# Full down projections of a hybrid encoder by a seven-product block scheme on one Trainium2 core

## The chip, the core and the metric

The kernel runs on one core of one Trainium2 chip (trn2). The metric is device time in microseconds: 1104.0 us before, the median of 3 runs (1103.97 to 1104.03). Every duration below is read from one profiled execution, unless it is said to be this median.

## What is computed

A bidirectional encoder trunk of two layers on 512 tokens of 1024 features in float32. The change touches the feed-forward half of a layer alone:

```python
h = _rmsnorm(x, g_ffn[l])
z = _dwconv_centred(h @ w_up[l], conv_w[l], conv_b[l])
z_gate, z_val = jnp.split(z, [D_FF], axis=-1)
x = x + (jax.nn.silu(z_gate) * z_val) @ w_down[l]
```

D_FF is 2816, 22 tiles of 128 features. The convolution is over three neighbouring tokens. The first half of a layer (projections, spatial gating, gated linear attention, output projection) and the final norm are as before.

## The kernel before

All activations lie feature-major: 128 features of a tile on the partitions, 512 tokens along them. A weight "slab" is 128 x 1024 float32, 8 blocks of 128 x 128, of which one projection tile needs a whole one. Every float32 product is three products in the type fp32r, high x high, high x low and low x high (`three`, lines 1042 to 1046), accumulated in one of four PSUM banks `acc0` to `acc3`. A slab goes through four slots j = 0 to 3, in this order: SP loads it to `w_raw` once the low part of the slab before it in the slot is made (`load_slab`); ACT copies it to `w_hi` (`split_hi`, line 348) once the array has finished with the slot; POOL subtracts (line 339) to get `w_lo` and counts `lo_done`; PE waits for `lo_done` and multiplies.

The 22 feature tiles are done in three parts: two full parts of 8 tiles and a last one of 6. A full part has 16 up slabs, in four groups of four (`up_quad` on ACT and DVE; two feature tiles each, gate and value), and then 8 down slabs, whose products are 8 blocks deep and 512 columns wide. Per up slab DVE scales the bank into `y` (line 940, a PSUM bank), ACT makes the centre tap (line 600), DVE adds the two outer taps (line 949). Per tile ACT takes the silu (line 608), DVE multiplies into `gated`, in PSUM (line 954), ACT copies it to `feat_hi` or `feat2_hi` (line 611) and DVE subtracts for the low part (line 931). Per down slab DVE adds the bank to `x` (`add_to_x`, line 915). `project_pair` interleaves the first two down slabs so that the last tiles' features are wanted late.

The order of each engine's work is written out by hand; semaphores with absolute counts tie the engines. Each engine takes its own instructions strictly in that order, so a wait holds back everything behind it on its engine.

In the printed source below, the projection's heart is:

```python
pe.matmul(out, wh, ah, start=first, stop=False)
pe.matmul(out, wh, al, start=False, stop=False)
return pe.matmul(out, wl, ah, start=False, stop=last)
```

## Time and profile before

| | |
|---|---|
| median of 3 runs | 1104.0 us (1103.97 to 1104.03) |
| span of the profiled execution | 1102.4 us |
| PE busy | 1092.6 us (99%), 5328 products |
| PE weight loads | 905.8 us (82%) |
| DVE busy | 531.0 us (48%) |
| ACT busy | 484.7 us (44%) |
| POOL busy | 464.8 us (42%) |
| HBM read | 105.98 MB, 98 GB/s over the span |

The profiled execution's own time is its span, first to last instruction of the program; it is 1.6 us below the median of the runs, which have the launch around it too. Busy time is the union of an engine's records; products overlap in the array, so two starts tell their pace and one record's length does not. Times in the timeline views count from the start of the span.

### The profile page before, as it was taken

To read this page: it belongs to the slowest core of one execution; us is meant where nothing else is said; L and a number is where in the kernel's file an instruction comes from. 1 tells how busy PE (TensorE), PEld (TensorE's weight loads), DVE (VectorE), ACT (ScalarE), POOL (GpSimd) and SP (SyncE) were. 2 spreads that over 40 slices of the span, in tenths; PEclk is the share of its full clock that TensorE was granted. 3 is DMA by queue.
4 is the path that set the end of the run, shared out by engine and by line. 5 is a ranking of instruction groups with operands and counts; after the bars stand their busy time and mean duration, and the time that the engine had idled before them with its cause. 6 is when DMAs were issued, how large, how long until landed. Compare 5 with 4: busy or idle time off the path is not lost.

```text
span 1102.4 us, 16315 instructions
## 1 busy us (share of the span) xinstructions
PE 1092.6 (99%) x5328; PEld 905.8 (82%) x5328; DVE 531.0 (48%) x816; ACT 484.7 (44%) x656; POOL 464.8 (42%) x202
## 2 busy tenths in 40 slices
PE   9999999999999999999999999999999999999997
PEld 7788888888888888888878888888888888888886
DVE  5726755655215551255536368456541355314545
ACT  7835444454225441344557344346432454313451
POOL 5334234344534443544634332435444444444450
PEclk9999999999999999999999999999999999999999
DMA  8222223232222222222522212222332322232222
GB/s 301 93 96 78 68 76 105 78 109 100 96 95 94 97 96 95 96 96 97 180 97 81 91 63 74 95 77 96 115 95 76 115 96 95 79 117 91 96 77 78
DMA packets 33607, 108.79 MB, mean 99 GB/s; under 512 B 3984, under 2 KB 6800, under 8 KB 33552
## 3 DMA queue, kind: packets, MB, share of 16 engines
q1 hardware_dynamic: 32848, 107.03, 29.2%
q10 hardware_dynamic: 704, 1.07, 0.3%
q8 instruction: 30, 0.49, 0.2%
q14 instruction: 25, 0.20, 0.1%
HBM read 105.98 MB, written 2.10 MB: 98 GB/s over the span
## 4 chain that ended last, share of the span: by engine, by line
PE 97%; DVE 1%; DMA 1%; ACT 0%; POOL 0%; SPq 0%; issue 0%; DVEq 0%
PE acc L1044 28%; PE acc L1045 28%; PE acc L1046 28%; PE acc L1170 3%; PE acc L1171 3%; PE acc L1172 3%; PE side L1140 1%; PE side L1258 1%; PE side L1242 1%; DMA x<-xT 1%; PE side L1248 1%; PE side L1221 1%; DVE arena L1019 1%; PE side L1201 1%; PE acc L1132 0%; PE acc L1121 0%
## 5 line engine op out<-in xcount | busy, mean ns | idle before, releaser
L339 POOL TENSOR_TENSOR w_lo<-w_raw,w_hi 128x1024 fp32r<-128x1024 f32 x188 | 453.4, 2416 | 600.6 <-ACT w_hi L348 600.6
L1044 PE MATMUL acc<-xg_hi,w_hi 128*128 128x512 f32 x864 | 338.8, 392 | 0.0
L1045 PE MATMUL acc<-xg_lo,w_hi 128*128 128x512 f32 x864 | 336.3, 389 | 0.0
L1046 PE MATMUL acc<-xg_hi,w_lo 128*128 128x512 f32 x864 | 336.2, 389 | 0.0
L348 ACT ACTIVATE w_hi<-w_raw 128x1024 fp32r<-128x1024 f32 x190 | 200.0, 1057 | 255.2 <-PE acc L1046 219.2
L1044 PEld LDWEIGHTS acc<-xg_hi,w_hi 128*128 128x128 f32 x864 | 162.2, 188 | 35.8 <-issue 2.0
L1046 PEld LDWEIGHTS acc<-xg_hi,w_lo 128*128 128x128 f32 x864 | 162.2, 188 | 33.9
L1045 PEld LDWEIGHTS acc<-xg_lo,w_hi 128*128 128x128 f32 x864 | 162.2, 188 | 33.5 <-issue 0.5
L1044 PE MATMUL acc<-feat_hi,w_hi 128*128 128x512 f32 (+1 forms) x492 | 188.9, 384 | 0.0
L1045 PE MATMUL acc<-feat_lo,w_hi 128*128 128x512 f32 (+1 forms) x492 | 188.8, 384 | 0.0
L1046 PE MATMUL acc<-feat_hi,w_lo 128*128 128x512 f32 (+1 forms) x492 | 188.8, 384 | 0.0
L949 DVE SCALAR_TENSOR_TENSOR arena<-side,conv_sb,arena 128x511 f32<-128x511 f32 x176 | 132.0, 750 | 116.8 <-ACT arena L600 104.0
L600 ACT ACTIVATE arena<-side,conv_sb 128x512 f32<-128x512 f32 x88 | 68.5, 778 | 127.7 <-DVE side L940 126.7
L915 DVE TENSOR_TENSOR x<-x,acc 128x512 f32 (+1 forms) x62 | 42.4, 685 | 167.8 <-PE acc L1046 167.8
L940 DVE TENSOR_TENSOR side<-acc,rstdT 128x512 f32<-128x512 f32 x88 | 61.4, 698 | 97.6 <-PE acc L1046 95.4
L1045 PEld LDWEIGHTS acc<-feat_lo,w_hi 128*128 128x128 f32 x492 | 92.4, 188 | 18.3
L1044 PEld LDWEIGHTS acc<-feat_hi,w_hi 128*128 128x128 f32 x492 | 92.4, 188 | 18.3
L1046 PEld LDWEIGHTS acc<-feat_hi,w_lo 128*128 128x128 f32 x492 | 92.4, 188 | 18.2
L611 ACT ACTIVATE feat_hi<-side 128x512 f32 (+1 forms) x44 | 26.4, 599 | 81.0 <-DVE side L954 81.0
L678 DVE SCALAR_TENSOR_TENSOR xg_lo<-x,gains_sb,xg_hi 128x512 fp32r<-128x512 f32 x32 | 41.5, 1306 | 29.6 <-ACT xg_hi L357 29.5
L1170 PE MATMUL acc<-w_hi,xg_hi 128*128 128x512 f32 x128 | 50.2, 392 | 0.0
L1171 PE MATMUL acc<-w_hi,xg_lo 128*128 128x512 f32 x128 | 49.8, 389 | 0.0
(131 smaller groups left out, 803.2 us busy)
## 6 DMA issues: line engine op xcount, KB each, us to landing
w_raw<-slabs SPq DMA_DIRECT2D x190, 512.0 KB, 3.3
outT<-arena SPq DMA_DIRECT2D x7, 256.0 KB, 2.3
ln_sb<-ln_gb SPq DMA_DIRECT2D x2, 512.0 KB, 7.7
w_raw<-slabs SPq DMA_DIRECT2D x4, 128.0 KB, 4.6
x<-xT ACTq DMA_DIRECT2D x2, 256.0 KB, 4.6
x<-xT SPq DMA_DIRECT2D x2, 256.0 KB, 5.9
x<-xT ACTq DMA_DIRECT2D x1, 512.0 KB, 7.2
w_raw<-slabs SPq DMA_DIRECT2D x2, 256.0 KB, 6.9
```

The source lines that it names most:

```text
L339: pool.tensor_tensor(w_lo[:, w], w_raw[:, w], w_hi[:, w].bitcast(F32), ALU.subtract).then_inc(lo_done, 1)
L348: act.activation(w_hi[:, w], w_raw[:, w], ACT.Copy).then_inc(hi_done, 1)
L600: act.activation(z[j], y[j], ACT.Identity, scale=conv_sb[:, bass.ds(coef + 1, 1)], bias=conv_sb[:, bass.ds(coef + 3, 1)]).then_inc(centre_ ...
L678: dve.scalar_tensor_tensor(out=xg_lo[:, w], in0=x[:, w], scalar=gains_sb[:, bass.ds(r * KT + m, 1)], in1=xg_hi[:, w].bitcast(F32), op0=ALU ...
L915: dve.tensor_tensor(x[:, bass.ds(m * S, S)], x[:, bass.ds(m * S, S)], acc[j][:, :], ALU.add).then_inc(x_done, 1)
L940: dve.tensor_tensor(y[j], acc[j][:, :], rstdT[:, :], ALU.mult).then_inc(y_ready, 1)
L949: dve.scalar_tensor_tensor(out=to, in0=of, scalar=conv_sb[:, bass.ds(coef + tap, 1)], in1=to, op0=ALU.mult, op1=ALU.add).then_inc(taps_don ...
L1044: pe.matmul(out, wh, ah, start=first, stop=False)
L1045: pe.matmul(out, wh, al, start=False, stop=False)
L1046: return pe.matmul(out, wl, ah, start=False, stop=last)
L1170: pe.matmul(acc[t][:, :], ah, wh, start=(k == 0), stop=False)
L1171: pe.matmul(acc[t][:, :], al, wh, start=False, stop=False)
```

## The change

The two full parts' down projections, in both layers, go through Strassen's scheme in Winograd's form. Eight down slabs are two quads of four. The host repacks each quad's weights (`quad_major`), so that its four slabs are the blocks of a 2 x 2 scheme: input tiles even or odd, output tiles of one or the other of a pair. The activations are split the same way: even and odd feature tiles, first and second half of the tokens (H = 256). Each quad then takes 7 "units" instead of 8 block products. A unit is 4 tile pairs x 2 output tiles x 3 products of 256 columns, 24 products; a part has 14 units, counted by `unit_done`. The second half of unit 4 and the last quarter of unit 3 are written apart: unit 4's first half stands before unit 3.

New operands have to be made:
- of the weights, per quad: S1 = block 1 + block 3, S2 = S1 - block 0, block 0 - block 1, S4 = block 2 - S2, each 128 x 1024. In the first quad POOL makes S1 and S2 and DVE the other two; in the second DVE makes all four. Each unit's block gets its own high part (ACT) and low part (POOL), so a part has 14 low parts in place of 8.
- of the features, per pair of tiles: T1 (DVE, from a copy that ACT makes, 256 columns), T2, T3, T4 (DVE, 256 columns each), a high part of T1 and one of T2 to T4 (ACT, 256 and 768 columns), and their low parts (DVE). The odd tile's low part and that of T2 to T4 stand behind the next pair's first scaling (`odd_low`); for the last pair they stand behind the first unit's addition.

S1 and S4 lie in `mixer_sb`, S2 in `sum_s2`. Blocks 1 and 3 of the second quad are loaded early into free places of `arena` (`second_raw`). DVE adds each finished unit into the one, two or four quarters of `x` that it belongs to (`add_unit`), some of them before the same bank goes on accumulating.

```diff
+        second_raw = {1: slot(4, 2), 3: slot(6, 2)}
+        t_raw, even_copy = slot(20, 2), slot(22)[:, 0:H]
...
+                    for j in second_raw:
+                        load(j, second_loaded[j])
                     for j in range(RING):
-                        load_slab(L, q, j)
+                        sp.wait_ge(lo_done, n + j + 1)
+                        if j in second_raw:
+                            sp.sem_inc(raw_loaded[j], 16)
+                        else:
+                            load(j, raw_loaded[j])
...
-            with pool.Fori(1, DEPTH * NS // RING) as q:
-                for j in range(RING):
-                    w = slice(j * SLAB, (j + 1) * SLAB)
-                    pool.wait_ge(hi_done, q * RING + (j + 1))
-                    pool.tensor_tensor(w_lo[:, w], w_raw[:, w], w_hi[:, w].bitcast(F32),
-                                       ALU.subtract).then_inc(lo_done, 1)
...
+            def low_quads(L, part):
+                m, slab = quads_at(L, part)
+                n = L * NS + slab
+                pool.wait_ge(hi_sum, 6 * m + 1)
+                low(0, raw(0)).then_inc(lo_sum, 1)
+                pool.wait_ge(raw_loaded[1], 16 * (n // RING) + 16)
+                pool.wait_ge(raw_loaded[3], 16 * (n // RING) + 16)
+                if m:
+                    pool.wait_ge(sum_done, 6 * m)
+                pool.tensor_tensor(sum_s1, raw(1), raw(3), ALU.add).then_inc(sum_done_pool, 1)
+                pool.wait_ge(sum_done_pool, 2 * m + 1)
+                pool.tensor_tensor(sum_s2[:, :], sum_s1, raw(0), ALU.subtract).then_inc(sum_done_pool, 1)
+                pool.wait_ge(hi_sum, 6 * m + 2)
+                low(1, sum_s1).then_inc(lo_sum, 1)
+                pool.wait_ge(hi_done, n + 1)
+                pool.wait_ge(sum_done, 6 * m + 2)
+                low(2, sum_s2[:, :]).then_inc(lo_done, 1)
+                pool.wait_ge(hi_sum, 6 * m + 3)
+                low(3, raw(2)).then_inc(lo_sum, 1)
+                pool.wait_ge(hi_done, n + 2)
+                low(0, raw(1)).then_inc(lo_done, 1)
+                pool.wait_ge(hi_done, n + 3)
+                low(1, sum_s4).then_inc(lo_done, 1)
+                pool.wait_ge(hi_done, n + 4)
+                low(2, raw(3)).then_inc(lo_done, 1)
...
+                    on_its_own(act)
+                    act.activation(even(H), t_raw[:, 0:H], ACT.Copy).then_inc(t_hi_done, 1)
+                    if down is None:
+                        next_hi(2)
+                    else:
+                        act.wait_ge(sum_done_pool, 2 * m + 2)
+                        unit_hi(2, sum_s2[:, :], hi_done)
+                    silu(1)
+                    if down is None:
+                        centre(1, 1)
+                        next_hi(3)
+                    else:
+                        act.wait_ge(acc_ready, L * NS + slab + RING)
+                        raw_at(2, first)
+                        unit_hi(3, raw(2), hi_sum)
+                        centre(1, 1)
+                        act.wait_ge(unit_done, 14 * m + 1)
+                        act.wait_ge(sum_done, 6 * m + 2)
+                        unit_hi(0, raw(1), hi_done)
+                    act.wait_ge(t_done, stage * 2 + 2)
+                    on_its_own(act)
+                    act.activation(odd, gated[1], ACT.Copy).then_inc(feat_hi_done, 1)
+                    act.activation(t_of, t_raw[:, H:4 * H], ACT.Copy).then_inc(t_hi_done, 1)
...
+                def odd_low(part, k):
+                    hi, lo = pair_parts(k)
+                    t_at = slice(k * 3 * H, (k + 1) * 3 * H)
+                    stage = L * (FULL_PARTS * KP) + part * KP + k
+                    dve.wait_ge(feat_hi_done, L * NF + part * KT + (KT + 2 * k + 2))
+                    dve.tensor_tensor(lo(S, S), gated[1], hi(S, S).bitcast(F32), ALU.subtract).then_inc(feat_ready, 1)
+                    dve.wait_ge(t_hi_done, stage * 2 + 2)
+                    dve.tensor_tensor(t_lo[:, t_at], t_raw[:, H:4 * H], t_hi[:, t_at].bitcast(F32),
+                                      ALU.subtract).then_inc(t_ready, 1)
...
+                    scale(0)
+                    if k:
+                        odd_low(part, k - 1)
+                    taps(0, 0)
+                    scale(1)
+                    taps(0, 1)
+                    gate(0)
+                    if k == KP - 1:
+                        dve.wait_ge(sum_done_pool, 2 * m + 2)
+                        dve.wait_ge(raw_loaded[2], 16 * (L * (NS // RING)) + 4 * first + 16)
+                        dve.tensor_tensor(sum_s4, raw(2), sum_s2[:, :], ALU.subtract).then_inc(sum_done, 1)
+                    scale(2)
+                    dve.wait_ge(feat_hi_done, L * NF + part * KT + (KT + 2 * k + 1))
+                    dve.tensor_tensor(lo(0, H), gated[0][:, 0:H], hi(0, H).bitcast(F32),
+                                      ALU.subtract).then_inc(feat_ready, 1)
+                    dve.wait_ge(even_copied, stage + 1)
+                    dve.tensor_tensor(t1, gated[0][:, H:S], even_copy, ALU.subtract).then_inc(t_done, 1)
+                    taps(1, 0)
+                    dve.wait_ge(t_hi_done, stage * 2 + 1)
+                    dve.tensor_tensor(lo(H, H), t1, hi(H, H).bitcast(F32), ALU.subtract).then_inc(t_ready, 1)
+                    scale(3)
+                    if k == KP - 1:
+                        dve.tensor_tensor(raw(1), raw(0), raw(1), ALU.subtract).then_inc(sum_done, 1)
+                    taps(1, 1)
+                    gate(1)
+                    dve.wait_ge(gated_done, f + 2)
+                    dve.tensor_tensor(t2, gated[1][:, H:S], t1, ALU.subtract).then_inc(t2_done, 1)
+                    dve.wait_ge(t2_done, stage + 1)
+                    dve.tensor_tensor(t4, gated[1][:, 0:H], t2, ALU.subtract)
+                    dve.tensor_tensor(t3, t2, gated[0][:, 0:H], ALU.subtract).then_inc(t_done, 1)
...
+                    add_unit(0, 0, 0, 0, units + 1, unit_added)
+                    odd_low(part, KP - 1)
+                    add_unit(0, 1, 1, 1, units + 2, unit_added)
+                    dve.wait_ge(second_loaded[1], 16 * m + 16)
+                    dve.wait_ge(second_loaded[3], 16 * m + 16)
+                    dve.wait_ge(lo_sum, 6 * m + 2)
+                    dve.tensor_tensor(sum_s1, second_raw[1], second_raw[3], ALU.add).then_inc(sum_done, 1)
+                    add_unit(0, 0, 1, 0, units + 3, unit_added)
+                    dve.wait_ge(raw_loaded[0], loads)
+                    dve.tensor_tensor(second_raw[1], raw(0), second_raw[1], ALU.subtract).then_inc(sum_done, 1)
+                    add_unit(0, 0, 0, 2, units + 4, x_done, added + 1)
+                    dve.wait_ge(sum_done, 6 * m + 3)
+                    dve.wait_ge(lo_done, n + 1 + RING)
+                    dve.tensor_tensor(sum_s2[:, :], sum_s1, raw(0), ALU.subtract).then_inc(sum_done, 1)
+                    add_unit(0, 0, 1, 1, units + 5, x_done, added + 3)
+                    dve.wait_ge(raw_loaded[2], loads)
+                    dve.wait_ge(sum_done, 6 * m + 5)
+                    dve.wait_ge(lo_done, n + 3 + RING)
+                    dve.tensor_tensor(sum_s4, raw(2), sum_s2[:, :], ALU.subtract).then_inc(sum_done, 1)
+                    add_unit(0, 1, None, 0, units + 6, x_done, added + 2)
+                    dve.wait_ge(x_done, L * NX + part * KT + (KT + RING + 3))
+                    add_unit(0, 1, 0, 2, units + 7, x_done)
...
+                def unit(bank, slot_of, pairs, moving, first):
+                    for k in pairs:
+                        for r in range(2):
+                            a = slot_of * SLAB + r * (SLAB // 2) + k * P
+                            xh, xl = moving(k)
+                            out = acc[bank][:, r * H:(r + 1) * H]
+                            pe.matmul(out, w_hi[:, a:a + P], xh, start=(first and k == 0 and r == 0), stop=False,
+                                      skip_group_check=True)
+                            pe.matmul(out, w_hi[:, a:a + P], xl, start=False, stop=False, skip_group_check=True)
+                            last = pe.matmul(out, w_lo[:, a:a + P], xh, start=False, stop=(k == KP - 1),
+                                             skip_group_check=True)
+                    return last
...
+                    pe.wait_ge(lo_sum, 6 * m + 1)
+                    pe.wait_ge(y_ready, ys + 1)
+                    pe.wait_ge(feat_ready, feats + KT - 1)
+                    unit(0, 0, every_pair, b11, True).then_inc(unit_done, 1)
+                    pe.wait_ge(lo_sum, 6 * m + 2)
+                    pe.wait_ge(y_ready, ys + 2)
+                    pe.wait_ge(t_ready, stages + 2 * KP - 1)
+                    unit(1, 1, every_pair, t1, True).then_inc(unit_done, 1)
+                    pe.wait_ge(lo_sum, 6 * m + 3)
+                    pe.wait_ge(y_ready, ys + 3)
+                    unit(2, 3, range(0, 2), b21, True)
+                    pe.wait_ge(lo_done, n + 1)
+                    pe.wait_ge(unit_added, 6 * m + 1)
+                    unit(0, 2, range(0, 3), t2, False)
+                    pe.wait_ge(t_ready, stages + 2 * KP)
+                    unit(0, 2, range(3, 4), t2, False).then_inc(unit_done, 1)
+                    pe.wait_ge(feat_ready, feats + KT)
+                    unit(2, 3, range(2, 4), b21, False).then_inc(unit_done, 1)
+                    pe.wait_ge(lo_done, n + 3)
+                    pe.wait_ge(unit_added, 6 * m + 2)
+                    unit(1, 1, every_pair, b22, False).then_inc(unit_done, 1)
+                    pe.wait_ge(unit_added, 6 * m + 3)
+                    unit(0, 0, every_pair, t3, False).then_inc(unit_done, 1)
+                    pe.wait_ge(lo_done, n + 4)
+                    pe.wait_ge(x_done, xs + 1)
+                    unit(2, 2, every_pair, t4, True).then_inc(unit_done, 1)
...
+    def quad_major(w, rows, m):
+        v = w[rows.start:rows.stop, m * P:(m + RING) * P].reshape(KP, 2, P, 2, 2, P)
+        return [v[:, odd, :, :, i].transpose(1, 2, 0, 3).reshape(P, SLAB) for odd in range(2) for i in range(2)]
```

**On POOL, at the first quad's start.** Before, one loop of four low parts runs from one end of the program to the other. A piece of it:

```order
L339 TENSOR_TENSOR w_lo<-w_raw,w_hi 128x1024 [waits hi_done]
L338 REGISTER_ALU
L339 TENSOR_TENSOR w_lo<-w_raw,w_hi 128x1024 [waits hi_done]
L335 REGISTER_ALU
L335 COMPARE_AND_BRANCH
```

Now, from the last pair of up tiles on:

```order
L399 TENSOR_TENSOR w_lo<-w_raw,w_hi 128x1024 [waits hi_sum]
L410 TENSOR_TENSOR mixer_sb<-w_raw 128x1024 [waits raw_loaded3,raw_loaded1]
L412 TENSOR_TENSOR sum_s2<-mixer_sb,w_raw 128x1024 [waits sum_done_pool]
L399 TENSOR_TENSOR w_lo<-mixer_sb,w_hi 128x1024 [waits hi_sum]
L399 TENSOR_TENSOR w_lo<-sum_s2,w_hi 128x1024 [waits sum_done,hi_done]
L399 TENSOR_TENSOR w_lo<-w_raw,w_hi 128x1024 [waits hi_sum]
L399 TENSOR_TENSOR w_lo<-w_raw,w_hi 128x1024 [waits hi_done]
L399 TENSOR_TENSOR w_lo<-mixer_sb,w_hi 128x1024 [waits hi_done]
L399 TENSOR_TENSOR w_lo<-w_raw,w_hi 128x1024 [waits hi_done]
```

The two sums stand between the low parts of units 1 and 2, and the low part of S2 (the fifth row) waits for `sum_done`, DVE's count of its own two sums.

**On DVE, in the last pair of up tiles, around the third tile's scaling.** Before:

```order
L954 TENSOR_TENSOR side1<-side0,arena 128x512 [waits silu_done]
L939 REGISTER_ALU
L940 TENSOR_TENSOR side2<-acc2,rstdT 128x512 [waits acc_ready]
L930 ISA
L931 ISA [waits feat_hi_done]
L931 TENSOR_TENSOR feat2_lo<-side1,feat2_hi 128x512
```

Now:

```order
L1220 TENSOR_TENSOR side1<-side0,arena 128x512 [waits silu_done]
L1230 ISA
L1231 ISA [waits sum_done_pool]
L1232 TENSOR_TENSOR mixer_sb<-w_raw,sum_s2 128x1024 [waits raw_loaded2]
L1203 REGISTER_ALU
L1204 TENSOR_TENSOR side2<-acc2,rstdT 128x512 [waits acc_ready]
L1234 REGISTER_ALU
L1235 TENSOR_TENSOR feat2_lo<-side1,feat2_hi 128x256 [waits feat_hi_done]
L1237 REGISTER_ALU
L1238 TENSOR_TENSOR arena<-side1,arena 128x256 [waits even_copied]
```

The sum S4 (line 1232), which waits for POOL's S2, has come between the gate of the first tile and the scaling of the third up slab.

## Rows read from the trace of the kernel before

**Rows 1.** The page: span, PE's busy time, chain by engine.

```profile
span 1102.4 us, 16315 instructions
...
PE 1092.6 (99%) x5328; PEld 905.8 (82%) x5328; DVE 531.0 (48%) x816; ACT 484.7 (44%) x656; POOL 464.8 (42%) x202
...
PE 97%; DVE 1%; DMA 1%; ACT 0%; POOL 0%; SPq 0%; issue 0%; DVEq 0%
```

**Rows 2.** Busy time by stretches (the first line names the columns).

```profile
core 0: us, PE busy (x) PEld busy (x) DVE busy (x) ACT busy (x) POOL busy (x), PEclk, DMA share, GB/s
...
234.13:277.66 43.53, 43.53 (x193) 36.04 (x192) 22.87 (x32) 18.61 (x24) 19.46 (x9) 1.00 0.29 97
277.66:321.18 43.52, 43.52 (x193) 36.04 (x192) 8.40 (x12) 9.53 (x10) 19.07 (x8) 1.00 0.30 100
```

**Rows 3.** Timeline of PE at 1081.8 (start, us, engine, line, tiles).

```profile
1081.77 0.39 PE L1046 MATMUL acc<-feat_hi,w_lo 128*128 128x512 f32 x1
1081.99 0.28 PE L1044 MATMUL acc<-feat_hi,w_hi 128*128 128x256 f32 x1
1082.11 0.28 PE L1045 MATMUL acc<-feat_lo,w_hi 128*128 128x256 f32 x1
```

**Rows 4.** Timelines of PE, DVE, ACT and POOL from 277.6 to 284.

```profile
277.66 0.39 PE L1044 MATMUL acc<-feat_hi,w_hi 128*128 128x512 f32 x1
...
277.86 0.70 DVE L940 TENSOR_TENSOR side<-acc,rstdT 128x512 f32<-128x512 f32 x1 [1.86 <-PE acc L1046]
279.80 1.64 DVE L949 SCALAR_TENSOR_TENSOR arena<-side,conv_sb,arena 128x511 f32<-128x511 f32 x2 [1.24 <-ACT arena L600]
281.56 0.70 DVE L954 TENSOR_TENSOR side<-side,arena 128x512 f32<-128x512 f32 x1
283.22 0.69 DVE L931 TENSOR_TENSOR feat_lo<-side,feat_hi 128x512 f32 x1 [0.96 <-ACT feat_hi L611]
...
278.88 0.78 ACT L600 ACTIVATE arena<-side,conv_sb 128x512 f32<-128x512 f32 x1 [2.24 <-DVE side L940]
279.56 1.04 ACT L348 ACTIVATE w_hi<-w_raw 128x1024 fp32r<-128x1024 f32 x1
282.46 0.60 ACT L611 ACTIVATE feat_hi<-side 128x512 f32 x1 [1.86 <-DVE side L954]
...
280.68 2.40 POOL L339 TENSOR_TENSOR w_lo<-w_raw,w_hi 128x1024 fp32r<-128x1024 f32 x1 [3.04 <-ACT w_hi L348]
```

**Rows 5.** Groups by line and shape, and the page's DMA row.

```profile
L339 POOL TENSOR_TENSOR w_lo<-w_raw,w_hi 128x1024 fp32r<-128x1024 f32 x188 | 453.4, 2416 | 600.6 <-ACT w_hi L348 600.6
...
L348 ACT ACTIVATE w_hi<-w_raw 128x1024 fp32r<-128x1024 f32 x190 | 200.0, 1057 | 255.2 <-PE acc L1046 219.2
...
L915 DVE TENSOR_TENSOR x<-x,acc 128x512 f32<-128x512 f32 x30 | 20.4, 681 | 36.7 <-PE acc L1046 36.7
...
L991 DVE TENSOR_TENSOR x<-x,acc 128x256 f32<-128x256 f32 x4 | 1.7, 420 | 0.7 <-PE acc L1046 0.6
...
w_raw<-slabs SPq DMA_DIRECT2D x190, 512.0 KB, 3.3
```

**Rows 6.** Timelines of DVE and POOL at 141 and at 158.

```profile
141.71 2.47 DVE L880 TENSOR_TENSOR feat_lo<-arena,feat_hi 128x512 fp32r<-128x512 f32 x1 [0.92 <-ACT feat_hi L553]
...
158.57 2.29 DVE L678 SCALAR_TENSOR_TENSOR xg_lo<-x,gains_sb,xg_hi 128x512 fp32r<-128x512 f32 x1 [1.26 <-ACT xg_hi L357]
...
161.38 0.67 DVE L915 TENSOR_TENSOR x<-x,acc 128x512 f32<-128x512 f32 x1
...
141.24 2.40 POOL L339 TENSOR_TENSOR w_lo<-w_raw,w_hi 128x1024 fp32r<-128x1024 f32 x1 [5.74 <-ACT w_hi L348]
...
157.91 5.22 POOL L339 TENSOR_TENSOR w_lo<-w_raw,w_hi 128x1024 fp32r<-128x1024 f32 x2 [7.92 <-ACT w_hi L348]
```

**Rows 7.** Busy time by stretches at the end, PE's timeline at the start.

```profile
1098.50:1100.00 1.50, 0.00 (x0) 0.00 (x0) 0.50 (x2) 0.00 (x0) 0.00 (x0) 1.00 1.03 340
1100.00:1102.40 2.40, 0.00 (x0) 0.00 (x0) 0.00 (x0) 0.00 (x0) 0.00 (x0) 0.51 0.32 105
...
1.64 1.70 PE L1088 MATMUL side<-ones_r 128*128 128x128 f32 x7
...
4.74 1.73 PE L1088 MATMUL side<-ones_r 128*128 128x128 f32 x14
```

More of the change, by code:

```diff
@@ L52 @@
 HALVES = (slice(0, S // 2), slice(S // 2, S))
+H = S // 2
+KP = KT // 2
+QUADS = KT // RING
 TAIL = (KT - 2, KT - 1)
@@ L243, in on_its_own, with raw, raw_of, quads_at @@
             eng.sem_inc(waits_passed, 1)
+        def raw(j):
+            return w_raw[:, j * SLAB:(j + 1) * SLAB]
+        def raw_of(g, j):
+            return second_raw[j] if g and j in second_raw else raw(j)
+        def quads_at(L, part):
+            return L * FULL_PARTS + part, part * PART + (N_FFN + 2 * KT)
         def load_x(eng, g):
@@ L334, in _, with low_slabs @@
                                    ALU.subtract).then_inc(lo_done, 1)
-            with pool.Fori(1, DEPTH * NS // RING) as q:
-                for j in range(RING):
-                    w = slice(j * SLAB, (j + 1) * SLAB)
-                    pool.wait_ge(hi_done, q * RING + (j + 1))
-                    pool.tensor_tensor(w_lo[:, w], w_raw[:, w], w_hi[:, w].bitcast(F32),
-                                       ALU.subtract).then_inc(lo_done, 1)
+            def low_slabs(L, first, end):
+                with pool.Fori(L * (NS // RING) + first // RING, L * (NS // RING) + end // RING) as q:
+                    for j in range(RING):
+                        pool.wait_ge(hi_done, q * RING + (j + 1))
+                        low(j, raw(j)).then_inc(lo_done, 1)
@@ L343, in _ @@
+            for L in range(DEPTH):
+                before = RING if L == 0 else 0
+                for part in range(FULL_PARTS):
+                    low_slabs(L, before, N_FFN + part * PART + 2 * KT)
+                    low_quads(L, part)
+                    before = N_FFN + (part + 1) * PART
+                low_slabs(L, before, NS)
         @block.scalar
@@ L966, in _ @@
+                with dve.Fori(0, FULL_PARTS) as part:
+                    for k in range(KP):
+                        up_pair(part, k)
+                    down_quads(part)
                 for q in range(LAST_TILES // 2):
@@ new lines, in part_of, with moving, t_part @@
+                def part_of(odd, half):
+                    def moving(k):
+                        w = slice(half * H, (half + 1) * H)
+                        return tuple(featT(hi, 2 * k + odd)[:, w] for hi in (True, False))
+                    return moving
+                def t_part(i):
+                    def moving(k):
+                        a = k * 3 * H + (i - 2) * H
+                        return t_hi[:, a:a + H], t_lo[:, a:a + H]
+                    return moving
+                b11, t1, b21, b22 = part_of(0, 0), part_of(0, 1), part_of(1, 0), part_of(1, 1)
@@ L1355, in _ @@
                     if part < FULL_PARTS:
-                        with pe.Fori(0, KT // RING) as q:
-                            for j in (1, 2, 3):
-                                down_tile(j, q, *places)
+                        down_quads(part)
                     else:
@@ L1447 @@
             rows = range(tiles.start * P, tiles.stop * P)
-            slabs += [channel_major(w_down[l], rows, m * P) for m in range(KT)]
+            if len(tiles) == KT:
+                for m in range(0, KT, RING):
+                    slabs += quad_major(w_down[l], rows, m)
+            else:
+                slabs += [channel_major(w_down[l], rows, m * P) for m in range(KT)]
     slabs = np.stack(slabs)
```

248 lines of the change are left out of this document (223 added, 25 removed).

## The prediction

> **What bounds the kernel now.** I read the page first: TensorE is busy 99% of a span of 1102.4 us and 97% of the chain that ended last is PE [rows 1]. The other engines have slack on average, so a change pays only through the array's own work or through a wait that it makes. Next, the busy time by stretches around the first full part's down projections in layer 0 [rows 2]: four pairs of up tiles end at 277.66, the eight down tiles take 277.66 to 321.18, 43.52 us, and the array never stops in either. 43.52 over 8 x 24 products is 0.2267 us for one of 512 columns; an up tile is 5.44 us. There are four such down stretches. POOL is busy only 19.07 of the 43.52 us, 8 low parts of 2.4 us. Then the array's own timeline where it goes from 512 to 256 columns [rows 3]: starts are 0.22 apart before and 0.12 after, while a record reads 0.39 and 0.28, so starts count.
>
> **The product saving.** The change replaces 192 products of 512 columns by 14 units of 24 products of 256 columns, 336. At the pitch of [rows 3] a unit is 24 x 0.12 = 2.88 us, a stretch 40.32 us: 3.20 us less than 43.52, 12.8 us over four. This is the whole gain; it would give 1091.2. The Trainium skill ("TensorE: Matmul & The Clock Gate", Back-to-back issue gap) gives N/2.4 + 2.5 ns, 215.8 and 109.2: by it the estimate would be 41.4 - 36.7 = 4.7 us a stretch. The rows have some 13 ns on top of N/2.4 at both widths, so shorter products gain less, and the rows decide.
>
> **Durations and handoffs.** POOL 2.42 mean for 1024 columns, ACT 1.06 for a high part, DVE 0.68 for 512 and 0.42 for 256 columns [rows 5]. I extrapolate DVE: 0.94 for 768, 1.20 for 1024. At the end of an up tile [rows 4] DVE begins 0.20 after the array, ACT 0.3 after DVE, DVE 0.14 after ACT, POOL 0.08 after ACT; centre 0.78, two taps 1.64, gate 0.70, low part 0.69.
>
> **The hold.** What this trace shows of DVE beside POOL decides the rest [rows 6]. A subtraction on DVE with both inputs in SBUF began at 141.71 while POOL was in an operation that began at 141.24 and took 2.40: it took 2.47 instead of 0.68, ending 0.54 after POOL. Another, from 158.57 to 160.86, ended 0.55 after POOL's first operation (157.91 + 2.4), and POOL's next ended later for it: the two read 5.22 together instead of 4.8. An addition with one input in PSUM, at 161.38 in the middle of a POOL operation, took its usual 0.67. So such a DVE operation and a POOL operation follow one another, whole. The new DVE work holds many of that kind: the block sums (1024 columns), T1's low part (256), the T2-T4 low part (768). I charge: wait for POOL's end, then the duration less 0.14; POOL's next starts behind it.
>
> **Entry into the first quad**, time 0 being the end of the last up tile (277.66 in the old trace).
> - The third pair ends late. Its fourth up tile ended at -21.76; scaling waits for T1's low part, itself held behind POOL's low part (about 0.7). Then centre, taps, gate as in [rows 4], and three new 256-column differences: -15.3. ACT makes the odd high part 0.60 and the T high part 0.83: -13.6. Centre and w_hi for unit 1, 0.78 + 1.05: -11.7.
> - POOL, in its new order, has four operations of 2.40: low of block 0 (-9.2), S1 (-6.8), S2 (-4.4), low of S1 (-2.0). The low of S1 stands ready behind S2, so POOL goes straight on.
> - DVE waits for S2 at the sum S4, and everything of the pair is queued behind. S2 exists at -4.4, but POOL is already in the low of S1: S4 ends at -2.0 + 1.06 = -0.9. The scaling of tile 3, due at -5.24, ends at -0.2; the even low part at 0.2 (unit 1 starts 0.3 late); T1 0.6; ACT's centre to 0.84; taps 2.6; T1's low 3.0; scaling of tile 4 3.7; raw0 - raw1 5.0.
> - POOL may take the low of S2 only after that difference: 7.5, then the low of raw2: 10.0. The array is through units 1 and 2 at 0.3 + 5.76 = 6.1 and needs the low of raw2: it goes on at 10.2. **Wait 4.1 us**, in sum 4.4.
> - Odd high part, T high part and, held once more, the T2-T4 low part end at about 13.2, due in unit 3's last quarter at 13.8; with no wait before it that would be due at 9.4, so it is next in line.
>
> **Through the quads.** From 5.2 POOL owes nine low parts before unit 10 (S2, raw2, raw1, S4, raw3; raw0, S1, raw2, S2): 21.6 us. Between them DVE puts the 768-column low part and four sums (held each time): 0.8 + 4 x 1.07 = 5.1; POOL saves 0.14 of its start at each, 0.7. Together 5.2 + 21.6 + 5.1 - 0.7 = 31.2. The array, at 2.88 a unit, reaches unit 10 at 30.3 and starts at 31.4: **1.1 us**. Behind it DVE has only additions from PSUM, POOL keeps a lead, and units 10 to 14 end at 31.4 + 14.4 = 45.8. Loads are 3.3 us [rows 5] and start at least 5 us ahead of their readers: nothing. The next up tile's low part is ready at about 41: nothing. The 144 more products a stretch on the array's queue are in the pitch.
>
> **Sum.** 45.8 - 43.52 = +2.3 us a stretch: -3.2 for the products, +4.4 entry, +1.1 unit 10. Times four, +9.1. The profiled execution's span goes from 1102.4 to 1111.5; the median is 1.6 above that span, so **1113.1 us**. Bounds: no wait at all gives -12.8 (1091.2); with each POOL hand-over and T step 0.3 later, +1.5 a stretch, 1119.
>
> **Rivals.**
> 1. *The forecast, waits larger than the saving.* For it: every duration has a row, and POOL's 26 us of work between the difference and unit 10 does not depend on who wins a race at entry. Against: the chain has some 25 steps, and 2.3 us fewer would make it nought. Chance 0.60, 1109 to 1118.
> 2. *DVE gets in between S2 and the low of S1.* Both are ready within 0.2 us of S2's end. If DVE is first, S4 ends at -3.2, 2.3 earlier; the difference, the nine low parts and unit 10 move with it, to 29.1, and the stretch ends at 43.5. Time 1104, between 1102 and 1106: no change. The Trainium skill ("SBUF — State Buffer", Who interferes with whom) says that whoever issues first has the shared ports for the whole instruction; by it this is settled by start order, and [rows 6] agree, with 2.47 us. Against: in the row of two POOL operations at 157.91 the second follows at once, while handoffs to DVE take 0.14 or more. Chance 0.13.
> 3. *Faster: the sums do not hold each other up.* If 1024-column sums pass beside POOL, S4 ends at -5.6, the difference at 2.1, raw2's low part at 6.9: wait 1.3, no second one, 42.0 a stretch: -6 in all, 1098. The point from which it decides is an entry wait below 3.2 us together with a free POOL. Against: both held rows. For: none of them has 1024 columns on DVE, and the pair before may end earlier than I chained it. Chance 0.20, 1092 to 1101.5.
> 4. *The clock falls in the entry gap.* The gap is about 4 us without a product, longer than any in the body of the old trace. Granted clock there: about 0.51 (1.2 GHz) in the stretch from 1100.0, after the array's last product at 1095.2 [rows 7]. At the start, 7 products read 1.70 us in the stretch at 1.64 and 14 read 1.73 later: half pace for some 3 us. Such an event costs about 1.6 us, up to 6.4 over four: 1115 to 1120. The gap of the forecast is shorter than those 4.8 us. Chance 0.07.
> That the change does not do what it says I rule out: the order of instructions shows 14 units and the seven-product scheme.
>
> **Numbers.** Two in ten are left out beyond 1100.0 and 1119.0. A measurement of this kernel tells 0.2%, 2.2 us, from no change. Faster 0.20 (rival 3), within 0.11 (most of rival 2), slower 0.69 (the rest). The forecast's own range is 1109 to 1118.
>
> **What would show it.** Right: in each of the four stretches one idle time of the array of about 4 us before the third block's products, ended by POOL's low part, and one of about 1 us at unit 10; 256-column starts 0.12 apart; DVE's first S4 sum reading over 3 us, and POOL over 30 us busy in a stretch, with records near 2.85 among its own. Wrong: DVE sums of 1.2 us beside POOL, an entry wait under 2 us, or the array ending a stretch in under 43 us. A pitch over 0.13 would put the loss into the products instead: 336 x 0.01 is 3.4 us a stretch.

## The result and the profile after

The changed kernel takes 1109.52 us, median of 4 runs (1109.07 to 1112.22), against 1104.01 us: ratio 1.0055, 95% interval 1.004 to 1.0069. Slower, inside the range and on the side forecast. The profiled execution is the longest of the four, 1112.22 us with a span of 1110.3, so what is read from its trace stands about 2.7 us above the median; what sets it apart turns out to matter.

The page of the changed kernel, answering to [rows 1]:

```profile
span 1110.3 us, 17568 instructions
...
PE 1090.2 (98%) x5904; PEld 932.7 (84%) x5904; DVE 666.3 (60%) x960; ACT 516.4 (47%) x720; POOL 553.8 (50%) x234
...
PEclk9999999999999999999999999999999999899999
...
issue 48%; POOL 32%; PE 14%; DVE 2%; ACT 1%; DMA 1%; POOLq 1%; DVEq 0%; SPq 0%; ACTq 0%
...
L1696 PE MATMUL acc<-feat_hi,w_hi 128*128 128x256 f32 x256 | 74.4, 291 | 12.2 <-POOL w_lo L399 12.2
```

TensorE is busy 2.4 us less than before in a span 7.9 us longer, and one line names the wait: 12.2 us of idle time before the products with a block's high part, ended by POOL's low part (line 399). The clock row shows a single slice below full. The chain, 97% PE before, has turned to "issue" and POOL. Its shares do not say that POOL sets the pace for a third of the time: TensorE waits for POOL's low parts 12.2 us in all, at those four places.

Busy time by stretches, the four down stretches of the changed kernel (the columns as in [rows 2], the clock behind the five engines):

```profile
277.24:322.54 45.30, 42.30 (x337) 41.89 (x336) 28.38 (x30) 17.34 (x19) 35.80 (x14) 0.96 0.26 83
409.61:455.24 45.63, 42.32 (x338) 41.91 (x337) 28.93 (x30) 17.32 (x19) 35.79 (x14) 0.96 0.25 82
821.72:867.82 46.10, 43.16 (x338) 42.95 (x337) 28.43 (x30) 17.32 (x19) 35.54 (x14) 0.93 0.25 81
954.88:1000.97 46.09, 43.14 (x338) 42.93 (x336) 28.67 (x30) 17.32 (x19) 35.53 (x14) 0.93 0.24 80
```

Each was 43.52 us long. Together they are 9.04 us longer, and the rest of the program is 1.1 us shorter. POOL is busy 35.5 to 35.8 us where it had 19.07. The clock column is the news: 0.96 and 0.93, in every one of them.

Units are counted here in the order in which TensorE takes them, so "the third" begins with the half of unit 4 that stands before unit 3. TensorE's timeline in the first stretch, where the second unit's last product starts at 282.88:

```profile
282.88 0.28 PE L1699 MATMUL acc<-feat_hi,w_lo 128*128 128x256 f32 x1
286.12 0.38 PE L1696 MATMUL acc<-feat_hi,w_hi 128*128 128x256 f32 x1 [2.97 <-POOL w_lo L399]
...
286.58 0.28 PE L1696 MATMUL acc<-feat_hi,w_hi 128*128 128x256 f32 x1
286.70 0.28 PE L1698 MATMUL acc<-feat_lo,w_hi 128*128 128x256 f32 x1
...
287.20 0.42 PE L1698 MATMUL acc<-feat_lo,w_hi 128*128 128x256 f32 x1
287.42 0.41 PE L1699 MATMUL acc<-feat_hi,w_lo 128*128 128x256 f32 x1
...
308.05 0.39 PE L1696 MATMUL acc<-t_hi,w_hi 128*128 128x256 f32 x1
```

Start to start the gap is 3.24 us, 3.12 more than the pitch of 0.12. Some 0.9 us after its end the starts are 0.21 apart for 17 products, then 0.12 again. At unit 10 (308.05) the start is 0.31 behind the one before: a wait of 0.19 us; in the last two stretches there is none. The granted clock in a piece at 1.2 GHz and on both sides of it (the same view by stretches):

```profile
282.90:286.80 3.90, 0.93 (x8) 0.73 (x7) 3.55 (x7) 1.27 (x3) 3.90 (x3) 1.00 0.44 139
286.90:290.25 3.35, 3.35 (x18) 3.35 (x17) 3.35 (x3) 0.90 (x1) 3.35 (x2) 0.50 0.02 5
290.30:293.70 3.40, 3.40 (x31) 3.40 (x31) 3.40 (x3) 1.06 (x1) 1.53 (x2) 1.00 0.29 64
```

It is 0.50, which is 1.2 GHz, for 3.41 us in each of the first two stretches, from 0.75 and 1.2 us after the gap on, and for 6.83 in each of the other two, where it fell 1.0 us before the gap's end: 20.5 us in all. Starts at 0.213 instead of 0.12 cost 1.5 us in each of the first two and about 2.6 in the others.

VectorE and GpSimd ahead of the gap (timelines of the changed kernel). On VectorE line 1232 is S4, 1204 a scaling and 1244 the difference of the first two blocks; on POOL line 410 is S1, 412 is S2 and 399 a low part:

```profile
272.25 3.17 DVE L1232 TENSOR_TENSOR mixer_sb<-w_raw,sum_s 128x1024 f32<-128x1024 f32 x1 [1.28 <-POOL sum_s L412]
275.34 0.68 DVE L1204 TENSOR_TENSOR side<-acc,rstdT 128x512 f32<-128x512 f32 x1
...
280.00 1.22 DVE L1244 TENSOR_TENSOR w_raw<-w_raw 128x1024 f32<-128x1024 f32 x1
...
264.75 2.40 POOL L399 TENSOR_TENSOR w_lo<-w_raw,w_hi 128x1024 fp32r<-128x1024 f32 x1 [3.57 <-ACT w_hi L726]
267.12 2.39 POOL L410 TENSOR_TENSOR mixer_sb<-w_raw 128x1024 f32<-128x1024 f32 x1
269.58 2.40 POOL L412 TENSOR_TENSOR sum_s<-mixer_sb,w_raw 128x1024 f32<-128x1024 f32 x1
271.95 2.39 POOL L399 TENSOR_TENSOR w_lo<-mixer_sb,w_hi 128x1024 fp32r<-128x1024 f32 x1
281.37 2.39 POOL L399 TENSOR_TENSOR w_lo<-sum_s,w_hi 128x1024 fp32r<-128x1024 f32 x1 [7.03 <-DVE w_raw L1244]
283.71 4.71 POOL L399 TENSOR_TENSOR w_lo<-w_raw,w_hi 128x1024 fp32r<-128x1024 f32 x2
```

This is the chain of the prediction, link by link: POOL goes from S2 straight on to the low part of S1 (271.95), S4 comes 0.30 later and is held to 3.17 us, the scaling stands behind it, then the difference of the first two blocks (280.00), and only then POOL's low part of S2 and the one that TensorE waits for (it ends near 286.05).

### The profile page after: what moved, and what is told of

Same layout as the page of the kernel before. It is cut to its first block, busy times and chain, and to the rows that moved or that the text cites. A ratio compares the mean times of both kernels' runs of the same rounds, so it can differ in the third digit from the quotient of the medians.

```text
span 1110.3 us, 17568 instructions
## 1 busy us (share of the span) xinstructions
PE 1090.2 (98%) x5904; PEld 932.7 (84%) x5904; DVE 666.3 (60%) x960; ACT 516.4 (47%) x720; POOL 553.8 (50%) x234
## 3 DMA queue, kind: packets, MB, share of 16 engines
q10 hardware_dynamic: 704, 1.07, 0.3%
## 4 chain that ended last, share of the span: by engine, by line
issue 48%; POOL 32%; PE 14%; DVE 2%; ACT 1%; DMA 1%; POOLq 1%; DVEq 0%; SPq 0%; ACTq 0%
POOL w_lo L399 30%; PE acc L1385 3%; PE acc L1386 3%; PE acc L1387 3%; PE acc L1696 2%; PE acc L1699 2%; PE acc L1698 2%; POOL sum_s L412 1%; POOL mixer_sb L410 1%; DMA x<-xT 1%; DVE arena L1213 1%; DVE arena L1360 1%; DVE side L1204 1%; DVE w_raw L1244 0%; POOL w_lo L389 0%
## 5 line engine op out<-in xcount | busy, mean ns | idle before, releaser
L1385 PE MATMUL acc<-feat_hi,w_hi 128*128 128x512 f32 (+1 forms) x236 | 89.3, 379 | 0.0
L1386 PE MATMUL acc<-feat_lo,w_hi 128*128 128x512 f32 (+1 forms) x236 | 89.3, 378 | 0.0
L1387 PE MATMUL acc<-feat_hi,w_lo 128*128 128x512 f32 (+1 forms) x236 | 89.3, 378 | 0.0
L1696 PE MATMUL acc<-feat_hi,w_hi 128*128 128x256 f32 x256 | 74.4, 291 | 12.2 <-POOL w_lo L399 12.2
L1264 DVE TENSOR_TENSOR x<-x,acc 128x512 f32<-128x512 f32 (+1 forms) x56 | 40.4, 721 | 64.7 <-PE acc L1699 64.7
L1699 PE MATMUL acc<-feat_hi,w_lo 128*128 128x256 f32 x256 | 74.0, 289 | 0.0
L1698 PE MATMUL acc<-feat_lo,w_hi 128*128 128x256 f32 x256 | 73.9, 289 | 0.0
L1696 PEld LDWEIGHTS acc<-feat_hi,w_hi 128*128 128x128 f32 x256 | 50.4, 197 | 13.1 <-POOL w_lo L399 13.0
L1696 PE MATMUL acc<-t_hi,w_hi 128*128 128x256 f32 x192 | 57.0, 297 | 0.1
L1698 PE MATMUL acc<-t_lo,w_hi 128*128 128x256 f32 x192 | 56.5, 295 | 0.0
```

Of the source, the lines that this page charges most:

```text
L1696: pe.matmul(out, w_hi[:, a:a + P], xh, start=(first and k == 0 and r == 0), stop=False, skip_group_check=True)
L1698: pe.matmul(out, w_hi[:, a:a + P], xl, start=False, stop=False, skip_group_check=True)
L1699: last = pe.matmul(out, w_lo[:, a:a + P], xh, start=False, stop=(k == KP - 1), skip_group_check=True)
```

## The experiments

All were timed beside the kernel before, which gave 1103.98 to 1104.08 us. "Time" is the median; stretches, waits and clock falls are those of the one profiled execution, which for the change is the 1112.22 us one. A "wait" is the distance of two starts less 0.12. 336 starts without any wait would take 40.32 us (336 x 0.12), and behind most waits the next start comes after 0.22 instead of 0.12, another 0.1 us each. Values are of the first stretch, with the one furthest from it where the others differ by over 0.1; "mean" is of all four stretches.

| kernel | time, us | ratio, 95% | mean stretch | entry wait | wait at unit 10 | clock falls in the four |
|---|---|---|---|---|---|---|
| before | 1104.0 | | 43.52 | none | | 0 |
| the change | 1109.52 | 1.004 to 1.0069 | 45.78 | 3.12 (to 3.45) | 0.19 (to 0) | 4 |
| 24 fillers | 1111.7 | 1.0056 to 1.0083 | 45.7 | filled, 5.27 | 0 | 0 |
| late S4 | 1100.02 | 0.995 to 0.9977 | 42.77 | 1.21 (to 1.56) | 0.96 | 0 |
| load waits | 1117.76 | 1.0108 to 1.0139 | 47.24 | 1.22 at the second unit, then 3.52 (to 3.28) | 0.39 (to 0) | 4 |
| both of these | 1106.76 | 1.0016 to 1.0036 | 44.42 | 2.58 (to 2.34) | 1.14 (to 0.27) | 2 |
| 12 fillers | 1107.78 | 1.0021 to 1.0046 | 44.70 | 3.17 (to 3.48), filled but for the last 0.49 | 0.96 | 0 |
| late S4, early difference | 1096.46 | 0.9918 to 0.9945 | 41.87 | 0.27 (to 0.60) | 1.05 | 0 |
| late S4, low part on DVE | 1097.64 | 0.9929 to 0.9957 | 42.17 | 1.22 (to 1.57) | 0.38 | 0 |
| all three | 1093.98 | 0.9895 to 0.9925 | 41.26 | 0.27 (to 0.60) | 0.48 | 0 |
| the change, sums on DVE | 1103.98 | 0.9991 to 1.0009 | 43.70 | 2.05 | 0.96 (0.19 in one) | 1 |
| all three, sums on DVE | 1098.21 | 0.9933 to 0.996 | 42.32 | 1.35 | 0.51 | 0 |

**Is it the clock? Fillers in the entry gap.** The changed kernel with products of `ones` that nobody reads, in front of the third unit's wait; 24 first:

```diff
+pe.wait_ge(y_ready, ys + 4)
+for _ in range(24):
+    pe.matmul(acc[3][:, 0:P], ones, ones, start=True, stop=True)
 pe.wait_ge(lo_sum, 6 * m + 3)
```

> The change, with 24 products of 128 columns of ones into the free bank acc3 between unit 2 and unit 4, so that the array is not idle in the entry gap (the output is the same; 24 x 0.112 = 2.7 us of the 3.1 us gap). Clock theory (a third or more of the loss is the array's clock, which the profile of the change shows at 0.5 for 3.4 or 6.8 us behind each gap): no drop of the granted clock in the four stretches, no start-to-start times of 0.213 us, each stretch 43.5 to 43.8 us instead of 45.3 to 46.1, time 1103.5 to 1105. Waits-only theory (the forecast's: the loss is the waits): same as the change, 1109 to 1110.

The filler was mis-sized. TensorE's timeline of this kernel:

```profile
282.97 5.52 PE L1739 MATMUL acc<-ones_r 128*128 128x128 f32 x48
288.24 0.36 PE L1696 MATMUL acc<-feat_hi,w_hi 128*128 128x256 f32 x1
```

Each filler is two records and 0.22 us, the third unit starts 2.1 us later than in the change (288.24 and 286.12), and TensorE then comes to unit 10 so late that it waits for nothing. Neither expectation holds. It shows one thing only: without a pause the clock does not fall. So again with 12:

> The changed kernel with 12 products of ones (not read by anything) on TensorE in the entry gap, between its third and fourth 256-column unit. The 24 of the longer filling took 5.3 us, so 12 should take about 2.65, less than the 3.1 us idle there. If the lower clock after the gap is what makes up the loss (theory): TensorE is idle for no more than 0.5 us at a stretch, the granted clock does not fall, each stretch takes 43.5 to 43.8 us (the 40.3 of its products, the gap of 3.1, the 0.1 to 0.3 of the tenth unit), time 1103.5 to 1105. If the waits alone make it up (rival): the stretches stay at 45.3 or over and the time at 1109.

(The gap lies ahead of the third unit; the expectation counts it one too late.) TensorE's timeline with 12 fillers, at the third unit and at unit 10, and behind it the first two stretches:

```profile
282.99 2.84 PE L1739 MATMUL acc<-ones_r 128*128 128x128 f32 x24
286.16 0.39 PE L1696 MATMUL acc<-feat_hi,w_hi 128*128 128x256 f32 x1 [0.33 <-POOL w_lo L399]
...
307.37 0.39 PE L1696 MATMUL acc<-t_hi,w_hi 128*128 128x256 f32 x1 [0.81 <-POOL w_lo L399]
```

```profile
277.24:321.87 44.63, 43.49 (x362) 43.10 (x361) 29.94 (x30) 17.38 (x19) 36.62 (x14) 1.00 0.25 84
408.93:453.88 44.95, 43.49 (x362) 43.09 (x360) 30.54 (x30) 17.34 (x19) 36.63 (x14) 1.00 0.24 83
```

The third unit starts at the same time as in the change (286.16 and 286.12), so the waits are untouched, and the clock stays at 1.00. The stretches come out between the two expectations, at 44.70 in the mean. Both expectations took over the change's wait at unit 10, 0.19 us or none; here it is 0.96. In the first stretch of the change TensorE, after its time at half pace, came to unit 10 1.45 us later than here, while the low part that it needs ended only 0.67 later (307.99 and 307.32). So the clock's fall costs less than its slow products: net 0.7 us after 3.41 us of it (45.30 - 44.63) and 1.5 after 6.83 (46.10 - 44.60). Of the +9.04 us of the profiled execution 4.7 are waits against savings and 4.3 the clock. The other three runs of the change have mean clocks of 0.994 and 0.995 where the profiled one has 0.989, and are 2.3 to 3.2 us shorter. By the medians, waits against savings make +3.8 us (1107.78) and the clock +1.7 (1109.52).

**Is it the hold of S4? S4 moved.** In the change it stands behind the first gating, in front of the third scaling; here behind T1's low part, in front of the fourth:

```diff
 gate(0)
-if k == KP - 1:
-    dve.wait_ge(sum_done_pool, 2 * m + 2)
-    dve.wait_ge(raw_loaded[2], 16 * (L * (NS // RING)) + 4 * first + 16)
-    dve.tensor_tensor(sum_s4, raw(2), sum_s2[:, :], ALU.subtract).then_inc(sum_done, 1)
 scale(2)
...
 dve.tensor_tensor(lo(H, H), t1, hi(H, H).bitcast(F32), ALU.subtract).then_inc(t_ready, 1)
+if k == KP - 1:
...
 scale(3)
```

> The change, with DVE's sum S4 moved from before the third scaling of the last pair to behind T1's low part, before the fourth scaling. Hold theory (S4, held behind POOL's low part of S1, sets the entry wait): S4 takes 1.2 us instead of 3.2, the entry wait falls from 3.1 to about 1.2 us, the clock does not drop, but POOL is then the bound up to unit 10 (26.6 us from the difference on, as in the change) and unit 10 waits about 1.5 us: 43.2 to 43.6 us a stretch, 1102.5 to 1104.5. Rival (POOL's own work sets the entry): entry wait stays near 3 us, 1108 to 1110.

Timelines of VectorE and POOL in this kernel:

```profile
271.91 0.70 DVE L1204 TENSOR_TENSOR side<-acc,rstdT 128x512 f32<-128x512 f32 x1 [1.04 <-PE acc L1387]
...
276.01 1.23 DVE L1241 TENSOR_TENSOR mixer_sb<-w_raw,sum_s 128x1024 f32<-128x1024 f32 x1
...
277.96 1.22 DVE L1244 TENSOR_TENSOR w_raw<-w_raw 128x1024 f32<-128x1024 f32 x1
...
271.85 2.42 POOL L399 TENSOR_TENSOR w_lo<-mixer_sb,w_hi 128x1024 fp32r<-128x1024 f32 x1
279.32 2.41 POOL L399 TENSOR_TENSOR w_lo<-sum_s,w_hi 128x1024 fp32r<-128x1024 f32 x1 [5.06 <-DVE w_raw L1244]
```

S4 (276.01) falls into a time when POOL is idle and takes 1.23 us instead of 3.17; the third scaling starts at 271.91 instead of 275.34, the difference 2.04 us earlier, and the entry wait is 1.91 us shorter. At 1.2 us the clock no longer falls, and the tenth unit waits its full 0.96. The time is 1100.02 us, below both kernels. Of the 9.5 us gained on the change 1.7 are the clock's, as the 12 fillers show; against these a stretch is 1.93 us shorter (44.70 and 42.77), all of it at the entry. It is also better than the 1102.5 to 1104.5 expected, which had the clock at full already: unit 10 was expected to wait about 1.5 us, and the program outside the four stretches is some 1 us shorter than before.

**Is it POOL's wait for the difference?** POOL may not take the low part of S2 before `raw0 - raw1` is made. The wait can be put on SP instead, ahead of a load:

```diff
-pool.wait_ge(sum_done, 6 * m + 2)
 low(2, sum_s2[:, :]).then_inc(lo_done, 1)
...
+sp.wait_ge(sum_done, 6 * m + 2)
```

> The change, with the wait for DVE's first two sums taken from POOL's low part of S2 and put before SP's load of the second quad's block 0, the other reader that it protects. Hold theory: POOL runs earlier but now holds DVE's T1 low part and the difference; the late feature chain (taps, gate, T parts) ends later, unit 3 waits for the first addition or for T2 to T4: one gap of 3 to 4.5 us again, at unit 3, time 1108 to 1112. Rival (the entry is only POOL's wait for DVE's difference): entry wait under 1 us, about 1101.

And the same together with the late S4:

> Both of the two edits before: S4 behind T1's low part, and the load instead of POOL waiting for the two sums. Hold theory: entry wait below 0.5 us, POOL starts its low parts about 1 us before the pair ends and is the bound only at unit 10, which waits about 1.2 us: 41.7 us a stretch, 1096 to 1099, faster than both kernels. Rival (POOL has no room for 14 low parts whatever the order): about 1102.

Both missed: 1117.76 us where 1108 to 1112 was expected, and 1106.76 where 1096 to 1099 was. TensorE and VectorE in the first, and below it VectorE and POOL in the second:

```profile
281.80 0.36 PE L1696 MATMUL acc<-feat_hi,w_hi 128*128 128x256 f32 x1 [1.07 <-DVE feat_lo L1241]
...
289.70 0.36 PE L1696 MATMUL acc<-t_hi,w_hi 128*128 128x256 f32 x1 [3.36 <-DVE x L1264]
...
279.58 2.08 DVE L1241 TENSOR_TENSOR feat_lo<-arena,feat_hi 128x256 fp32r<-128x256 f32 x1
...
282.18 2.81 DVE L1244 TENSOR_TENSOR w_raw<-w_raw 128x1024 f32<-128x1024 f32 x1
```

```profile
279.50 2.82 DVE L1244 TENSOR_TENSOR w_raw<-w_raw 128x1024 f32<-128x1024 f32 x1
...
278.59 2.64 POOL L400 TENSOR_TENSOR w_lo<-w_raw,w_hi 128x1024 fp32r<-128x1024 f32 x1 [1.04 <-ACT w_hi L726]
```

Free to start early, POOL's low parts now lie across T1's low part (2.08 us, 0.43 in the last pair of the change) and the difference (2.8, 1.22 in the change), and the last pair's features come late. In the first, TensorE waits 1.22 us at unit 2 for T1's low part; the clock falls four times. The wait ahead of the third unit is gone in both kernels, but 12 products later, in front of unit 3, TensorE waits 3.52 and 2.58 us for VectorE's first addition, which stands behind the whole last pair. The wait that was taken away had kept POOL out of VectorE's way.

**The difference early instead.** With the late S4, `raw0 - raw1` right behind the first gating:

```diff
 gate(0)
+if k == KP - 1:
+    dve.wait_ge(sum_done_pool, 2 * m + 1)
+    dve.tensor_tensor(raw(1), raw(0), raw(1), ALU.subtract).then_inc(sum_done, 1)
 scale(2)
```

> The late S4 (as in the run that moved it alone) and besides the difference of the first two blocks right behind the first gating on VectorE, so that GpSimd's low part of S2, which waited 5.06 us for that difference there, finds it done. Theory: the entry wait falls from 1.3 us to 0.4 or less, the tenth unit's wait of 1.1 us stays or grows by what the entry gives up (to at most 1.6), stretch 42.2 to 42.7, time 1098 to 1100.2. Rival: the early difference meets GpSimd's S2 or low part of S1 and is held some 3 us, which delays the scalings of the last pair: a wait in front of the stretch of 0.5 to 2 us and a time of 1101 to 1106.

Timelines of VectorE and POOL:

```profile
270.78 2.22 DVE L1231 TENSOR_TENSOR w_raw<-w_raw 128x1024 f32<-128x1024 f32 x1
...
269.51 2.41 POOL L412 TENSOR_TENSOR sum_s<-mixer_sb,w_raw 128x1024 f32<-128x1024 f32 x1
...
278.36 2.41 POOL L399 TENSOR_TENSOR w_lo<-sum_s,w_hi 128x1024 fp32r<-128x1024 f32 x1 [3.09 <-DVE mixer_sb L1244]
```

The difference is held by POOL's S2 as the rival says, but for 1 us only, where VectorE had 1.04 idle: it takes 2.22 us, and the scaling behind it starts at 272.93 instead of 271.91. The entry wait is 0.27 us, and unit 10 waits 1.05, hardly more than the 0.96 with the late S4 alone, since POOL's whole chain has moved forward: its low part of S2 is now released by S4 and starts at 278.36 instead of 279.32. The time, 1096.46 us, is below both ranges, since unit 10 took up almost nothing of what the entry gave up.

**The tenth unit's low part on VectorE.** With the late S4 alone, and with both other edits:

```diff
+dve.wait_ge(hi_done, n + 5)
+dve.tensor_tensor(w_lo[:, 2 * SLAB:3 * SLAB], sum_s2[:, :],
+                  w_hi[:, 2 * SLAB:3 * SLAB].bitcast(F32), ALU.subtract).then_inc(low_by_dve, 1)
...
-low(2, sum_s2[:, :]).then_inc(lo_done, 1)
+pool.wait_ge(low_by_dve, m + 1)
+pool.sem_inc(lo_done, 1)
```

> The late S4, and besides the low part of the second quad's S2 (the tenth unit's) on VectorE in place of GpSimd, so that GpSimd has one 1024-column operation less behind which the tenth unit's weights wait. Theory: the tenth unit's wait of 1.1 us goes, the entry's 1.3 stays, stretch 41.6 to 41.9, time 1095.5 to 1097.5. Rival: VectorE's operation reads two tiles of SBUF as well and is held by GpSimd's queue of low parts, so that the order of the two only turns round: the tenth unit still waits 1 us or more and the time stays at 1099.5 to 1101.

> All three together: late S4, early difference of the first two blocks, the tenth unit's low part on VectorE. Theory: both waits go, what is left is 40.3 us of products and under 0.6 us of waits, stretch 40.5 to 41.0, four stretches 10 to 12 us shorter than before the change, time 1092 to 1094.5. Rival: a third wait comes in their place (the fourteenth unit or the first up tile behind the stretch), and the time is no better than with the low part on VectorE alone, 1095.5 to 1097.5.

Timelines of TensorE and VectorE with all three edits:

```profile
303.89 0.36 PE L1702 MATMUL acc<-t_hi,w_hi 128*128 128x256 f32 x1 [0.32 <-DVE x L1267]
...
301.64 1.50 DVE L1298 TENSOR_TENSOR w_lo<-sum_s,w_hi 128x1024 fp32r<-128x1024 f32 x1
303.07 1.27 DVE L1267 TENSOR_TENSOR x<-x,acc 128x512 f32<-128x512 f32 x2
```

The low part takes 1.50 us there, but the additions queue behind it and unit 10 now waits for one of them to free its bank: 0.38 to 0.48 us are left of 0.96. That is why the first of the two, with 1097.64 us and 42.17 a stretch, is just over its ranges; the second is inside its range of time, its stretch of 41.26 a little over. Together the three give 1093.98 us, ratio 0.991: the version to keep, 10.0 us below the kernel before.

**The first sums back on VectorE.** S1 behind the second scaling, S2 behind the first gating, POOL without either; in the change and in the best version:

> The changed kernel with its first two sums back on VectorE: S1 behind the second scaling of the last pair, S2 behind its first gating, S4 behind that as in the change. GpSimd makes low parts alone. Theory (the loss starts where GpSimd's chain of block 0's low part, S1, S2 and the low part of S1 meets VectorE's S4): VectorE's three sums cost 1.2 us each where GpSimd is idle, S4 ends near 273.3 to 274.5 us instead of 275.4, GpSimd's low part of S2 starts 1 to 2 us earlier than 281.37, the entry gap is 1 to 2.2 us instead of 3.2, the clock does not fall, time 1101 to 1106. Rival: the low part of S1, now free to start earlier, runs across S2 and S4 and holds one of them for 2 us or more, so that the third scaling of the last pair is no earlier; gap 3 us or more, the clock falls as before, time 1108 to 1112.

> The version with the late S4, the early difference and the tenth unit's low part on VectorE, and besides the first two sums on VectorE. It has entry waits of 0.25 us (0.6 in the second stretch) and 0.45 us at the tenth unit left. Theory that GpSimd's lateness is all that the entry waits for: the entry wait goes, the tenth unit's stays, stretch 40.9 to 41.1, time 1093 to 1094. Rival: three sums in a row on VectorE (3.6 us where 1.9 us are idle) make the last pair's scalings late, the last up tile or the first unit waits 0.5 us or more in front of each stretch, time 1095 to 1099.

VectorE in the first:

```profile
267.22 1.22 DVE L1223 TENSOR_TENSOR mixer_sb<-w_raw 128x1024 f32<-128x1024 f32 x1
...
270.94 2.15 DVE L1229 TENSOR_TENSOR sum_s<-mixer_sb,w_raw 128x1024 f32<-128x1024 f32 x1
273.13 1.23 DVE L1233 TENSOR_TENSOR mixer_sb<-w_raw,sum_s 128x1024 f32<-128x1024 f32 x1
274.27 0.69 DVE L1197 TENSOR_TENSOR side<-acc,rstdT 128x512 f32<-128x512 f32 x1
```

Only S2 is held (2.15 us), the scaling starts 1.07 us earlier than in the change, and the entry wait is 1.07 us shorter. The time is that of the kernel before. The clock was expected to stay up; it fell once in the four gaps of 2.05 us. In the best version the same move costs 4.2 us, as the rival says: there is no held S4 to save, and the entry wait goes from 0.27 to 1.35. So in this kernel GpSimd is the better place for the first sums, once S4 is out of the way.

## Why the prediction came out right, and what in it was not

- **Products:** right. Starts are 0.12 apart, so 336 take the 40.32 us charged. What the sum left out is the 0.22 us between the first two starts behind a wait, 0.1 us each time. The Trainium skill ("TensorE: Matmul & The Clock Gate", Back-to-back issue gap) gives 109.2 ns for this width; no row here has it.
- **The hold:** right, with the value it had been given: S4 took 3.17 us ("over 3 us" in the prediction) and POOL was busy 35.8 us in a stretch (over 30). The operations of POOL that stand behind a held one read 3.12 to 3.38 us in the first stretch, not "near 2.85". Moving S4 alone turned 3.17 into 1.23 us. Rival 2 did not happen: POOL's low part of S1 began at 271.95, S4 at 272.25. The Trainium skill ("SBUF — State Buffer", Who interferes with whom) lets whoever issues first keep the shared ports for its whole instruction; the trace agrees, with these two starts.
- **Rival 3's sum:** wrong in itself. It has S4 end at -5.6, before the S2 that it reads is there (-4.4); without any hold it would end near -3.2, as in rival 2, and the entry wait of 1.3 us worked out from it would be about 1.9.
- **Entry, the term that was mis-sized:** right in kind, 4.4 us forecast, 3.12 measured. Of the 1.3 us between them 0.9 are there before S4. Counted from the end of the last up tile (277.24), unit 1's high part was to be ready at -11.7 and was at -12.6; POOL's block 0 at -9.2 and -10.1; the low part of S1 at -2.0 and -2.9; S4 at -0.9 and -1.8; the difference at 5.0 and 4.0; TensorE at 10.2 and 8.9. The step that failed is "the third pair ends late". The scaling started 0.5 us after its up tile, not 0.7, and the rest adds up ACT's and VectorE's operations and handoffs in full, while neighbouring records overlap by about 0.1 us each (ACT's four from 261.72 end at 264.68, 2.96 us where their records add up to 3.27). The other 0.4 lie between S4's end and TensorE's start, 10.7 us where 11.1 were charged; unit 1 did not start late.
- **Unit 10:** 1.1 us forecast, 0.96 where the clock stays up. From the end of the difference to unit 10 the prediction has 26.4 us (5.0 to 31.4); with 12 fillers it is 26.1 (281.26 to 307.37). In the change itself only 0.19 us or nothing shows, since the slow products had covered the rest.
- **The clock, rival 4, chance 0.07:** this happened in all four stretches. "The gap of the forecast is shorter than those 4.8 us" was no reason: gaps of 3.1 to 3.45 were enough each time. Its price of 1.6 us a fall is about what the slow products took in two of the four (1.5; 2.6 in the others), but net it was 0.7 and 1.5 us, because a later wait shrank by the rest.
- **The sum:** without the clock a stretch is 44.70 us, not 45.8, +1.2 instead of +2.3. By the medians, from 1113.1 forecast to 1109.5 measured, the stretches took off 4.5 us, the program outside them another 0.9, which no term has, and the clock put 1.7 back; the profiled execution, where the clock was low longest, took 1112.2. The mechanism and the direction stand: with the clock kept up the kernel is still slower than before, by 3.8 us. That the time lies inside the forecast's range of 1109 to 1118 is luck: with the clock kept up it was 1107.8, below the range, and only the event that the prediction gave 0.07 brought it in.
- **Not tried:** the part that loads half of the second quad's blocks early was never undone by itself.

## What to carry to other kernels

Before a summation goes onto VectorE beside a busy GpSimd, look at which of its inputs lie in SBUF and where the other engine's operations will lie in time: moving one 1.2 us sum further down the queue gave 9.5 us, 1.7 of them through the clock. Removing a wait can cost more than it gives where the wait had kept two such operations apart, so look at what the freed engine will run across. And a pause of TensorE of some microseconds is to be priced with the products behind it at 1.2 GHz, less what later waits then lose.
